# Norm sums of queries and keys as two rounded products, in a two-block transformer kernel on one core

## The reference, cut to what matters

```python
def rms_norm_2(x, g):
    y = xf * lax.rsqrt(jnp.mean(xf * xf, axis=-1, keepdims=True) + EPS)
    return (y * g.astype(jnp.float32)).astype(x.dtype)
...
proj = h @ w_in[l]
gq, gk, gv, gr, glr, aq, ak, av = jnp.split(proj, split_at, axis=-1)
...
qa = rms_norm_2(aq.reshape(B, S, ATTN_HEADS, ATTN_HEAD_DIM), q_norm_g[l])
ka = rms_norm_2(ak.reshape(B, S, ATTN_HEADS, ATTN_HEAD_DIM), k_norm_g[l])
y_att = dilated_attention_group(qa, ka, av.reshape(B, S, ATTN_HEADS, ATTN_HEAD_DIM))
```

## Time and profile before

| what | value |
|---|---|
| median of three runs | 1373.43 us |
| the profiled execution's own time | 1373.26 us |
| span of its trace | 1371.6 us |
| PE busy | 1355.8 us, 99% of the span |
| DVE busy | 881.1 us, 64% |
| ACT busy | 589.4 us, 43% |
| granted TensorE clock | full (1.0, 2.4 GHz) |
| instructions in the trace | 19384 |

### The profile page before, as it was taken

How to read it: one execution, slowest core, us unless ns; L and a number is a source line. 1 busy time by engine, 2 the same in 40 slices (tenths; PEclk the granted TensorE clock), 3 DMA queues, 4 the chain that set the end, 5 groups by cost and what they waited for, 6 DMA issues and landing times.

```text
span 1371.6 us, 19384 instructions
## 1 busy us (share of the span) xinstructions
PE 1355.8 (99%) x6846; PEld 1106.6 (81%) x6846; DVE 881.1 (64%) x1479; ACT 589.4 (43%) x984; POOL 57.5 (4%) x119
## 2 busy tenths in 40 slices
PE   9999999999999999999999999999999999999999
PEld 7777777778988888888887688777798888888887
DVE  6667676678777777774337977766576566565221
ACT  5455545554452323323223735666354444443221
POOL 0000000000001211120100000000000000000000
PEclk9999999999999999999999999999999999999999
DMA  6222212213315555555443112111212322233332
GB/s 208 92 77 77 75 64 77 77 62 123 103 63 192 194 196 191 192 188 172 128 142 118 47 62 77 62 62 63 77 58 92 103 95 92 98 101 115 87 97 88
DMA packets 42871, 147.08 MB, mean 107 GB/s; under 512 B 5440, under 2 KB 5952, under 8 KB 42816
## 3 DMA queue, kind: packets, MB, share of 16 engines
q1 hardware_dynamic: 34848, 120.37, 27.0%
q0 software_dynamic: 7824, 25.70, 5.6%
q10 hardware_dynamic: 144, 0.26, 0.1%
HBM read 143.69 MB, written 2.10 MB: 106 GB/s over the span
## 4 chain that ended last, share of the span: by engine, by line
PE 90%; DVE 6%; ACT 2%; issue 1%; DMA 0%; DVEq 0%; SPq 0%; ACTq 0%; POOLq 0%
PE bank L664 60%; PE bank L844 13%; PE bank L682 4%; PE bank L783 3%; PE bank L870 2%; PE bank L960 2%; PE bank L891 1%; PE bank L909 1%; PE bank L1130 1%; DVE w_lo L1940 1%; PE bank L912 1%; ACT w_hi L1326 0%; DVE xT L2442 0%; DVE xT L2255 0%; PE bank L1251 0%
## 5 line engine op out<-in xcount | busy, mean ns | idle before, releaser
L1940 DVE TENSOR_TENSOR w_lo<-raw,w_hi 128x1024 fp32r<-128x1024 f32 (+1 forms) x223 | 266.6, 1196 | 154.4 <-ACT w_hi L1326 153.5
L1326 ACT ACTIVATE w_hi<-raw 128x1024 fp32r<-128x1024 f32 (+1 forms) x223 | 230.5, 1035 | 287.3 <-PE bank L664 262.1
L664 PE MATMUL bank<-h_hi,w_hi 128*128 128x512 f32 x864 | 343.4, 397 | 3.2 <-DVE h_lo L2489 1.3
L664 PE MATMUL bank<-h_hi,w_lo 128*128 128x512 f32 x864 | 336.7, 390 | 0.0
L664 PE MATMUL bank<-h_lo,w_hi 128*128 128x512 f32 x864 | 336.5, 389 | 0.0
L664 PEld LDWEIGHTS bank<-h_hi,w_hi 128*128 128x128 f32 x864 | 162.1, 188 | 43.5 <-issue 3.9
L664 PEld LDWEIGHTS bank<-h_hi,w_lo 128*128 128x128 f32 x864 | 162.2, 188 | 34.3
L664 PEld LDWEIGHTS bank<-h_lo,w_hi 128*128 128x128 f32 x864 | 162.3, 188 | 33.9 <-issue 1.7
L664 PE MATMUL bank<-f_hi,w_lo 128*128 128x512 f32 x352 | 136.9, 389 | 0.0
L664 PE MATMUL bank<-f_hi,w_hi 128*128 128x512 f32 x352 | 136.9, 389 | 0.0
L664 PE MATMUL bank<-f_lo,w_hi 128*128 128x512 f32 x352 | 136.9, 389 | 0.0
(11 more groups left out here) (366 smaller groups left out, 1936.2 us busy)
## 6 DMA issues: line engine op xcount, KB each, us to landing
raw<-in_w_up SPq DMA_DIRECT2D x66, 512.0 KB, 3.3
ada<-in_w_ada POOLq DMA_DIRECT2D x96, 256.0 KB, 3.1
raw<-in_w_mix SPq DMA_DIRECT2D x47, 512.0 KB, 3.3
raw<-in_w_down SPq DMA_DIRECT2D x32, 512.0 KB, 3.5
raw<-in_w_in SPq DMA_DIRECT2D x24, 512.0 KB, 3.2
raw<-in_w_gate SPq DMA_DIRECT2D x22, 512.0 KB, 3.3
raw<-in_w_out SPq DMA_DIRECT2D x16, 512.0 KB, 3.2
raw<-in_w_down SPq DMA_DIRECT2D x16, 384.0 KB, 3.3
```

The source lines that it names most:

```text
L664: last = pe.matmul(to[:, :], wt[:, slot, k, :], act_[:, rhs0 + k, :], start=(k == first and n == 0), stop=(k == K - 1 and n == 2))
L1326: act.activation(w_hi[:, s, k0:K, :], raw[:, s, k0:K, :], ACT.Copy).then_inc(hi_ready[s], 1)
L1940: dve.tensor_tensor(w_lo[:, s, k0:K, :], raw[:, s, k0:K, :], w_hi[:, s, k0:K, :].bitcast(F32), ALU.subtract).then_inc(split_ready[s], 1)
```

## The change

For the dilated rounds 8 to 10 each norm sum is made of two rounded products in place of one plain float32 product: ACT squares the bank a second time into a rounded tile `qk_hi` (with its own wait for completion), DVE writes the remainder `qk_lo = qk_sq - qk_hi` (`square_rest`, in the place of `qk_sq` in memory), and PE adds `blk` by `qk_hi` and `blk` by `qk_lo`. PE waits for the remainder by a new semaphore count, `sq_split`. `blk` is declared as fp32r; the sums before round 8 read it as float32. In the table for rounds of 24 steps the query sum moves from after step 10 to after step 12, and the key sum from after step 18 to after step 19, right ahead of the last turn.

```diff
-DILATED_TURNS = {24: (4, 9, 11, 15, 19, 20), 21: (3, 8, 8, 13, 13, 18)}
+DILATED_TURNS = {24: (4, 9, 13, 15, 20, 20), 21: (3, 8, 8, 13, 13, 18)}
...
-        blk = sb("blk", [P])
+        blk = sb("blk", [P], F32R)
...
+        (qk_lo,), _ = region(gla_end, ("qk_lo", [2, S], F32R))
+        (_, _, qk_hi), _ = region(tmp_at, ("hbuf_too", [2, S], F32), ("sq_first", [S], F32), ("qk_hi", [S], F32R))
...
-                pe.matmul(S1[:, :], blk[:, :], qk_sq[:, m, :], start=True, stop=True).then_inc(qk_ms, 1)
+                pe.matmul(S1[:, :], blk[:, :].bitcast(F32), qk_sq[:, m, :], start=True, stop=True).then_inc(qk_ms, 1)
...
                 pe.wait_ge((q_staged, k_staged)[m], p + 1)
                 pe.wait_ge(qk_rs[0], p + 1) if m else pe.wait_ge(vd_ready, p)
-                pe.matmul(O1[:, :], blk[:, :], qk_sq[:, m, :], start=True, stop=True).then_inc(qk_ms, 1)
+                pe.wait_ge(sq_split, 2 * p + m)
+                pe.matmul(O1[:, :], blk[:, :], qk_hi[:, :], start=True, stop=False)
+                pe.matmul(O1[:, :], blk[:, :], qk_lo[:, m, :], start=False, stop=True).then_inc(qk_ms, 1)
...
                 then(act.activation(qk_sq[:, 0, :], dilated_bank(p, 0)[:, :], ACT.Square))
+                if p:
+                    then(act.activation(qk_hi[:, :], dilated_bank(p, 0)[:, :], ACT.Square))
                 act.activation(next_q[:, :], dilated_bank(p, 0)[:, :], ACT.Copy).then_inc(q_staged, 1)
...
                 then(act.activation(qk_sq[:, 1, :], dilated_bank(p, 1)[:, :], ACT.Square))
+                if p:
+                    then(act.activation(qk_hi[:, :], dilated_bank(p, 1)[:, :], ACT.Square))
                 act.activation(next_k[:, :], dilated_bank(p, 1)[:, :], ACT.Copy).then_inc(k_staged, 1)
...
+            def square_rest(p, m):
+
+                dve.wait_ge((q_staged, k_staged)[m], p + 1)
+                dve.tensor_tensor(qk_lo[:, m, :], qk_sq[:, m, :], qk_hi[:, :].bitcast(F32), ALU.subtract).then_inc(sq_split, 1)
+
             for i in range(8, 12):
...
                 store_turned(i, 0)
                 if i < 11:
+                    square_rest(p + 1, 0)
                     split_lo(0)
                 pair_logits(i, 3)
...
                 if i < 11:
                     dilated_distances(p + 1, 0)
+                    square_rest(p + 1, 1)
                     dilated_distances(p + 1, 1)
                     split_lo(1)
                     normed_k(p + 1)
```

More of the change, by code:

```diff
@@ L366, in build @@
         first_half_hi, first_half_lo = signal("first_half_hi"), signal("first_half_lo")
-        first_sq, first_sum = signal("first_sq"), signal("first_sum")
+        first_sq, sq_split = signal("first_sq"), signal("sq_split")
         first_half_in, first_x_in = signal("first_half_in", 16), signal("first_x_in", 16)
@@ L522, in _ @@
                                     base=0, pattern=[[-1, P]], channel_multiplier=1))
-            for t, v in ((blk, 0.0), (eps6, NORM_EPS), (eps5, SUBLN_EPS)):
+            then(pool.memset(blk[:, :].bitcast(F32), 0.0))
+            for t, v in ( (eps6, NORM_EPS), (eps5, SUBLN_EPS)):
                 then(pool.memset(t[:, :], v))
-            then(pool.memset(blk[0:64, 0:64], 1.0))
-            then(pool.memset(blk[64:128, 64:128], 1.0))
+            then(pool.memset(blk[0:64, 0:64].bitcast(F32), 1.0))
+            then(pool.memset(blk[64:128, 64:128].bitcast(F32), 1.0))
             pool.drain().then_inc(const_ready, 1)
@@ L804, in _ @@
             pe.wait_ge(const_ready, w.next(const_ready))
-            pe.wait_ge(first_sum, 1)
+            pe.wait_ge(sq_split, 1)
             pe.matmul(T1[:, :], ones[:, :], sqacc[:, :], start=True, stop=True).then_inc(ms_ready, 1)
@@ L2008, in _ @@
             then(dve.tensor_tensor(gate_b[:, 0:2, :], gate_b[:, 0:2, :], gate_b[:, 2:4, :], ALU.add))
-            dve.tensor_tensor(sqacc[:, :], gate_b[:, 0, :], gate_b[:, 1, :], ALU.add).then_inc(first_sum, 1)
+            dve.tensor_tensor(sqacc[:, :], gate_b[:, 0, :], gate_b[:, 1, :], ALU.add).then_inc(sq_split, 1)
             dve.wait_ge(lam_in, w.next(lam_in))
```

## The result

The changed kernel took 1376.83 us (median of 20 runs, 1375.11 to 1378.67), the kernel before 1374.27 us beside it (20 runs, 1372.92 to 1375.42): the ratio is 1.0018, 95% interval [1.0011, 1.0025], some 2.5 us or 0.18% slower. Forecast was 1375.2 us in a range of 1373.5 to 1376.6, so the time lies just above the range. The direction and the place were right. What was missing shows in the single runs, and it takes two traces to see it.

A forecast was written before the change was run, and what follows sets the result against it. PE was taken to bound rounds 8 to 10; its waits for the key remainder, net of cheaper products, lengthen them by 0.89 + 0.44 + 0.44 = 1.77 us, giving a median of 1375.2 us, range 1373.5 to 1376.6.

The forecast's parts named there:

- PE bounds these rounds, and a shift reaches the end whole: Rounds 8 to 10: PE is busy nearly throughout, so its shift at round 10's end reaches the kernel's end whole.
- The price of the products: Each norm sum on PE: two rounded products take 0.46 us in place of 0.87, saving 0.41, six sums 2.5 us.
- What ACT and DVE add, and that it is not lost again: Each sum adds 0.63 us on ACT (second Square) and 0.69 on DVE (remainder); ACT's 0.63 carries through the following links.
- The wait before the key sum: PE waits for DVE's key remainder, queued behind the first distance table: 1.16 us in round 9, where it had not waited.
- The rounds: Rounds 8, 9 and 10 get 0.89, 0.44 and 0.44 us longer, lasting 25.4, 26.2 and 26.2 us.
- rival 1: Key remainder wait at least 0.4 us shorter; scores wait for DVE's last turned copy instead: +0.5 us, 1374.0; chance 0.12.
- Rival 2: PE does not wait at all in these rounds, remainder and squares being much cheaper: -3.0 us, 1370.4; chance 0.06.
- Rival 3: Dear pair: the two rounded products cost 0.87 us, like the plain one, behind the key wait: +3.0 us, 1376.4; chance 0.08.
- After a wait a sum costs some 0.1 more: PE's restart at the key sum adds 0.10 us, read from round 8's earlier 0.47 us wait (1.65 against 1.56 us).
- The base: Starting time to which the sum was added: the kernel before at a median of 1373.43 us.

The follow-up runs named there:

- run without remainder: Changed kernel without DVE's square_rest and PE's wait for it, the second product multiplying blk with the rounded squares again: 1373.17 us, ratio 0.9993 to the kernel before.
- reordered kernel: Changed kernel with the key sum one step behind the last turn and last turned copies ahead of what waits: 1372.77 us; with 15 start fillers 1372.48 us.
- the new places alone: Kernel before with only the new DILATED_TURNS places (query sum after step 12, key sum after 19), sums still plain float32: 1372.80 us, ratio 0.9990.
- With the start filled: Changed kernel with 15 in place of 11 filler matmuls at the start (keep_clock): 1375.91 us; the kernel before with the same filler: 1373.59 us.
- products alone: Changed kernel with the old DILATED_TURNS places, so rounded products in the old places: 1377.71 us, ratio 1.0029 to the kernel before.
- changed again: Changed kernel, unaltered, timed once more beside the kernel before on one chip: 1376.64 us.

## Why the prediction was right or wrong, point by point

- **PE bounds these rounds, and a shift reaches the end whole: right.** 2.86 us of start and 1.99 us of rounds are 4.85; the two profiled executions differ by 4.82 (1378.08 - 1373.26).
- **The price of the products: right.** From 916.88 to 917.83 are 0.95 us against 1.33, a saving of 0.38 per sum (0.41 forecast). The rival with a dear pair falls.
- **What ACT and DVE add, and that it is not lost again: right.** 0.63 us per Square, 0.69 us per remainder. DVE's scaling of the queries starts 18.57 us after the scores of its round (902.27 to 920.84), before 17.94 (898.46 to 916.40): the 0.63 us of the one Square came through.
- **The wait before the key sum: right in place and cause, 0.12 us short in size.** The profile's 1.12 us look like the 1.16 forecast, but they count from the end that it shows for the last matmul (922.83 + 0.39). The forecast counted from when PE could have gone on, 0.23 us behind that matmul's start (923.06), and so counted the wait is 1.28 us. In round 8 the profile has 2.24 us idle. It was DVE's `qk_lo` that ended it, with the table and the copy of the keys both done just before it, as the sum had it. The run without remainder shows the two parts: 0.30 us left for the copy, 0.8 for the remainder.
- **The rounds: 0.95, 0.52 and 0.52 us longer against 0.89, 0.44 and 0.44 forecast.** 1.99 in place of 1.77: from the sum's start to the turn passed 0.54 us (0.56 forecast), but PE started 0.15 us behind the end of the remainder where I had put 0.04.
- **The rivals.** The scores' wait for DVE never came last (rival 1). Rival 2 did not happen; the reordered kernel shows how much of it was to be had, 1.1 us of 3.0 (rounds of 24.30, 25.37 and 25.37 us against 24.56, 25.80 and 25.80), and 0.7 of that comes with the new places alone. Rival 3 fell.
- **The step that failed is "After a wait a sum costs some 0.1 more".** I priced PE's wait by its length and a restart read from a wait of 0.47 us in the earlier trace rows. The wait of round 8 is near five times as long, and a fall of the granted clock behind it stood nowhere in my sum. With the start filled 6 of 13 executions were below full clock, and the trace of one shows the lower level right behind this wait: 1.6 us more (1377.27 against 1375.65 us, medians of the runs below and at full clock). In the profiled run of the changed kernel it had not fallen there, so neither that trace nor the one before shows it.
- **The base was mis-sized too.** I added 1.77 to the median of three runs, 1373.43, and let it wander by 0.5 us. Two of those three are, by their times, of the group at full clock; over 20 runs the kernel before has a median of 1374.27, since in a good part of its executions the start is late and costs 1.3 us. That alone puts the forecast at 1376.0. The median of 1374.27 is itself a matter of luck: none of the 20 runs took between 1373.95 and 1374.59 us, ten are on either side, and it is the middle of that gap. Like with like, at full clock, the difference is 1.8 us in one session (1375.53 against 1373.71) and 2.06 with the start filled, against 1.77 forecast and 1.99 read from the trace: there the forecast sum stands.

The median lies 1.63 us over the forecast. The base makes 0.84 of it and the rounds 0.22, which would still have been 1376.3 and in the range. The rest, some 0.6, is left for the falls of the clock behind the wait; no run measures that share by itself. It can be put only roughly: in the slower group by their times were 39 of 87 runs of the kernel before (the start), and below full clock 6 of 13 of the changed kernel with the start filled (the wait). If the two are independent, one or the other would meet 70% of the runs of the changed kernel; 18 of 31 took over 1376.5 us (58%).

## What to carry to other kernels

An operation made cheaper on the busiest engine is paid for by those that prepare its operands: walk the whole queue of each helper, and ask what its new instruction stands behind, before counting the saving. Price a new wait of TensorE not by its length alone; look for a longer idle stretch of the same kernel (here the start) and what the granted clock did behind it. And where single runs fall into two groups, find out which group the base belongs to before adding a fraction of a per cent to it. Group them by their times too, and check the record of the clock against the distances between equal matmuls.

## What the runs showed of the hardware that I had not expected

- The granted clock can fall to the lower level in the middle of a kernel that is otherwise 98% busy on PE, after one idle stretch of 2.23 us, and stays there for some 3.7 us (895.5 to 899.2 in the one trace that has it). The mean clock was below full in 6 of 13 executions of that program; 1.28 us of filler products ahead of the wait, which left 1.12 us idle, kept it up in 11 of 11.
- At the start 4 more filler products, which left PE idle for 0 to 0.81 us ahead of the first real product, kept it up in 44 of 44 runs of four kernels, and cost nothing: 1373.59 us against 1373.7 at full clock without them.
- Without them the length of the idle stretch at the start does not tell by itself whether the clock falls: the products came at the lower level behind 1.23, 1.79 and 2.55 us (products alone, reordered, changed) and at the full one behind 1.01, 1.19, 1.57 and 1.65 us (no remainder, changed again, place alone, before).
- The record of the granted clock can miss such a stretch: in the run with the products alone it says 1.00 where equal products stand 0.43 us apart in place of 0.23.
